# Mixer of a two-layer decoder step on one core: sample selection ahead of the prompt heads, layer norm moved, tanh for silu, rotations on TensorE

## The chip, the core and the metric

One core of a Trainium2 chip runs the whole step as one program. TensorE (PE) multiplies, VectorE (DVE), ScalarE (ACT) and GpSimd (POOL) work elementwise, SyncE (SP) issues most of the transfers; they run side by side and wait for each other through semaphores. The metric is the device time of one execution in microseconds (us); less is better. Three runs of the kernel before took 1205.79, 1207.03 and 1207.75 us (median 1207.03).

## The reference

Two layers work on 264 tokens: 256 of a prompt and one new token of each of 8 sequences ("samples") whose past of 1024 tokens lies in paged caches. Each layer is a gated feed-forward (SwiGLU), a mixer, and a second feed-forward, all with norms around them. Cut to the mixer, which is what changes:

```
a = u @ w_in                       # q, k, v, indexer q/k/weights, conv and pool inputs
q, k, qi, ki = partial_rope(...)   # x*cos + permuted(x)*sin
# convolution: depthwise, 31 taps, then
y = silu(layernorm(conv + bias)) @ conv_pw
# pooling: running means, then @ pool_w
# attention, prompt: indexer scores, top 64 of 256 per query, softmax over those, @ v
# attention, sample: indexer scores over 1025 keys, top 256, softmax over those, @ v
y = concat([conv, pool, attention]) @ w_out
```

All arithmetic is float32.

## The kernel before, in words

Activations lie transposed, features on the partitions, 264 tokens on the free axis, so one matrix unit is a 128x1024 tile of weights. Each such unit is loaded by SP into `raw`, rounded by ACT (`split`, L351) into `w_hi` and its rest computed by DVE (L556) into `w_lo`; PE then does three products for each of 8 blocks (L1001, L1002, L1003), 24 matmuls for one unit. A feed-forward has 66 units. The mixer has 16 units of input (numbers 0 to 15, of which 15 holds `conv_pw` and `pool_w`) and 8 of output.

The order of the work is written out by hand, once for each engine: each has a function `mixer(L)`, executed for both layers, and each engine works strictly through its own list. In the mixer:

- **Projections.** PE computes units 0 to 14 (`unit(m)`), DVE scales each by `rstd` as it leaves PSUM (`chunk`, L645). For the rotations PE multiplies the scaled tile by a permutation (`perm`, L1103), and DVE computes product with sine, product with cosine and sum (`rope`, L658, L659, L662). Between the units run the indexer scores and the search for the 256 largest of the 1025 sample scores, eight rounds of count on DVE (`count`, L716, L717) and sum over partitions on PE (`digit`, L1108).
- **Convolution.** 31 taps as small matmuls (`taps`, L1120) into four banks of PSUM, copied by ACT (L458) and added by PE (`fold`, L1131).
- **Attention.** The past keys come in two halves, `keys(0)` and `keys(1)` (L1235), because the tile `kv` holds 4 of 8 sequences; the second half can be loaded only when PE has used the first (semaphore `k_used`). The values are `values(0)` from a tile `vx` and `values(1)` from `kv` (L1324). The prompt's 8 heads go in four rounds j of two heads: `scores(j)` on PE (L1248, L1249), `masked(j)` on DVE (L859 to L863), `exps(j)` on ACT (L471), `norm(j)` on DVE (L870), transposes on PE (L1271), copies on ACT (L485), the product with the values on PE (L1282, L1283), and two copies out on ACT and DVE (L487, L892).
- **After the four rounds** come the layer norm of the convolution (L1297, L1301, L930, L932), the softmax over the sample's scores (L919 to L928, L491), transposes (L1308), the values, the silu (L501), the products with `conv_pw` and `pool_w`, and the output matrix: `half_out(0)` and `half_out(1)` first with 4 of 8 blocks each, the rest once the attention is there.

SP's list around the attention: when unit 14 is done, 8 transfers of values for one sequence into `vx` (`first_values`, L265), 32 of keys into `kv` (`batch`, L252, wait for `k_used`), 8 more into `vx`, 32 of values into `kv`, and then weights again. POOL issues 16 more transfers into `vx` (L1454) and computes the pooling.

Of the kernel before, what the change touches and what calls it, by code (L numbers as in the profile page):

```python
# [14 lines left out]
AL = mybir.AluOpType  # L15
# [67 lines left out]
    tanh=2, glu=2, stack=1, diag=2, conv=1, c_part=4, c_fold=1, conv_p=1, c_sum=1, c_cent=1, c_sq=1, c_var=1, c_rms=1, c_norm=1, c_silu=1,  # L83
# [9 lines left out]
def build(nc, xT, wts, par, cst, ptab, digits, kT, vC, kxT, scT, spT,  # L93
          yT, okT, ovT, okiT, ocP, ocS, opP, opS):
    ctx = ExitStack()
    with ctx:
# [20 lines left out]

        s1 = [at[0] + 4 * KD * NT]
# [33 lines left out]

        qi = place("qi", [128, 2, NT], F32, s1)
# [18 lines left out]
        rtmp = place("rtmp", [128, 2, NT], F32)  # L172
# [3 lines left out]
        kn = place("kn", [128, 4], F32)  # L176
        best = place("best", [128, 8], F32)
# [49 lines left out]
        CONV_BANKS = (3, 4, 5, 7)  # L227
# [9 lines left out]
        def _(sp):  # L237
# [42 lines left out]
            for L in range(DEPTH):  # L280
# [65 lines left out]
        def _(act):  # L346
# [69 lines left out]
            def mixer(L):  # L416
# [6 lines left out]
                for m in range(3, 7):  # L423
                    split(L, u0 + m)
                tanh(0)
# [18 lines left out]
                split(L, u0 + 11)  # L444
                act.wait_ge(sem["v_t"], at_layer(L, "v_t", 1))
                act.activation(vn[:, :, :], PS[:, 6, 128:384].rearrange(
                    "p (a b) -> p a b", a=2), ACT.Copy).then_inc(sem["v_nat"], 1)
                for m in range(12, 18):
                    split(L, u0 + m)

# [13 lines left out]
                ins.then_inc(sem["conv_p"], 1)  # L464

# [10 lines left out]
                exps(0)  # L476
                for j in range(4):
                    if j < 3:
                        exps(j + 1)
                    for a in range(2):  # L480
                        act.wait_ge(sem["p_t"], at_layer(L, "p_t", 2 * j + a + 1))
                        if j:

                            act.wait_ge(sem["o_p"], at_layer(L, "o_p", j))
                        act.activation(pT[:, a, :], PS[:, (7, 0)[a], 0:384], ACT.Copy).then_inc(sem["p_tc"], 1)  # L485
                    act.wait_ge(sem["o_p"], at_layer(L, "o_p", j + 1))
                    act.activation(h_hi[:, 4 + j, 0:NP], PS[:, 1, 0:NP], ACT.Copy).then_inc(sem["o_hi"], 1)  # L487
                act.wait_ge(sem["c_cent"], at_layer(L, "c_cent", 1))
                act.activation(csq[:, :, :], cacc[:, :, :], ACT.Square).then_inc(sem["c_sq"], 1)
                act.wait_ge(sem["s_smax"], at_layer(L, "s_smax", 1))  # L490
                act.activation(psm[:, :], psm[:, :], ACT.Exp, scale=SCALE,  # L491
                               bias=smx[:, 1:2], accum_out=smx[:, 2:3]).then_inc(sem["p_sexp"], 1)
                act.wait_ge(sem["c_var"], at_layer(L, "c_var", 1))
                act.activation(crs[:, :], PS[:, 1, 0:NT], ACT.Sqrt, scale=1.0 / 256, bias=epsb[:, 0:1]).then_inc(sem["c_rms"], 1)
                act.wait_ge(sem["p_st"], at_layer(L, "p_st", 1))
                act.activation(pTs[:, :, :].rearrange("p c (q r) -> p c q r", q=4),
                               PS[:, 6:8, :].rearrange("p a b -> p (a b)").rearrange(
                                   "p (c q x) -> p c q x", c=NPG, q=4)[:, :, :, 0:16], ACT.Copy).then_inc(sem["p_stc"], 1)
                act.wait_ge(sem["c_norm"], at_layer(L, "c_norm", 1))
                for c in range(2):  # L500
                    ins = act.activation(cacc[:, c, :], cacc[:, c, :], ACT.Silu,  # L501
                                         scale=pars[:, LNG + c:LNG + c + 1], bias=pars[:, LNB + c:LNB + c + 1])
                ins.then_inc(sem["c_silu"], 1)
                act.wait_ge(sem["c_silu"], at_layer(L, "c_silu", 1))
                act.activation(cp_hi[:, :, :], cacc[:, :, :], ACT.Copy).then_inc(sem["c_hi"], 1)
                act.wait_ge(sem["pool_y"], at_layer(L, "pool_y", 1))
                act.activation(pl_hi[:, :, :], pw[:, :, :], ACT.Copy).then_inc(sem["pl_hi"], 1)
                act.wait_ge(sem["c_out"], at_layer(L, "c_out", 1))
                act.activation(h_hi[:, 0:2, :], PS[:, 4:6, 0:NT], ACT.Copy).then_inc(sem["c_ohi"], 1)
                act.wait_ge(sem["unit_done"], at_layer(L, "unit_done", u0 + N_IN))  # L510
                for c in range(2):
                    ins = act.activation(h_hi[:, 2 + c, :], PS[:, 6 + c, 0:NT], ACT.Copy,
                                         scale=pars[:, PSC + c:PSC + c + 1])
                ins.then_inc(sem["pl_ohi"], 1)
                act.wait_ge(sem["v_used"], at_layer(L, "v_used", 2))
                for q in range(4):
                    ins = act.activation(osb[32 * q:32 * q + 8, :, :], PS[32 * q:32 * q + 8, 2:4, 0:128], ACT.Copy)
                ins.then_inc(sem["o_sc"], 1)
                split(L, u0 + 18)
                act.wait_ge(sem["o_ms"], at_layer(L, "o_ms", 1))  # L520
                act.activation(h_hi[:, 4:8, NP:], ms[:, :, :], ACT.Copy).then_inc(sem["o_shi"], 1)
# [26 lines left out]
        def _(dve):  # L548
# [88 lines left out]
            def mixer(L):  # L637
                u0 = U_MIX
                perms, ropes = [0], [0]
# [11 lines left out]
                def rope(x, bank, own=None):  # L651

                    perms[0] += 1
# [952 lines left out]
```

## Time and profile before

| | |
|---|---|
| runs, us | 1205.79, 1207.03, 1207.75 |
| the profiled execution, us | 1206.3 |
| its span (first to last instruction), us | 1204.8 |
| mean granted clock of TensorE | 0.96 |
| busy, share of the span | PE 92%, PEld 87%, DVE 64%, ACT 45%, POOL 17% |

A timeline row gives start, length, engine, line of the kernel, operation, what is written and read, how many instructions, and in brackets how long the engine stood idle before it and what released it. PE is recorded twice, as matmuls (PE) and as weight loads (PEld). An f32 matmul is recorded as two instructions, one on float32r data (a rounded part) as one. PEclk is the granted clock in parts of full speed: 1.00 is 2.4 GHz, 0.50 is 1.2 GHz. The first layer's mixer runs from 221.3 to 389.5 us, the second's from 811.5 to 979.7 us.

### The profile page before, as it was taken

What the parts mean: (1) busy time and instruction counts of PE and PEld (TensorE: products, weight loads), DVE (VectorE), ACT (ScalarE), POOL (GpSimd) and SP (SyncE); (2) the same over time, 40 slices, a digit from 0 to 9 for tenths busy, and PEclk for the clock granted to TensorE, in tenths of its full rate; (3) what the DMA queues carried; (4) which work ended last, traced back from release to release, by engine and by line L of the source; (5) the groups of instructions that cost most, each with busy time, mean ns of one, the idle gap of its engine ahead of it and who ended that gap; (6) DMA issues with size and microseconds to landing.
All of it is one profiled execution on the core that took longest, in us unless ns stands there. A gap on an engine that the chain in (4) does not pass through costs nothing.

```text
span 1204.8 us, 28977 instructions
## 1 busy us (share of the span) xinstructions
PE 1104.7 (92%) x9500; PEld 1044.8 (87%) x9500; DVE 774.2 (64%) x1244; ACT 541.6 (45%) x866; POOL 209.2 (17%) x233
## 2 busy tenths in 40 slices
PE   5999999978679999999989999999786799999997
PEld 4999999867348899999989999998663699999996
DVE  3766644789954766664466666457998466666546
ACT  4444434532345544443454444345223555444436
POOL 3211100210510312110031111011215021211002
PEclk9999999998869999999999999999896799999999
DMA  7454566343454355555435456553425434555551
GB/s 248 170 202 174 194 230 226 113 132 103 94 141 138 105 175 185 181 186 181 158 91 195 175 197 225 204 192 113 127 80 116 131 123 158 177 188 177 188 175 39
DMA packets 92302, 192.96 MB, mean 160 GB/s; under 512 B 12338, under 2 KB 50418, under 8 KB 92098
## 3 DMA queue, kind: packets, MB, share of 16 engines
q1 hardware_dynamic: 89730, 187.44, 46.9%
q0 software_dynamic: 2496, 4.55, 1.6%
q8 instruction: 42, 0.69, 0.2%
q14 instruction: 34, 0.28, 0.1%
HBM read 189.35 MB, written 2.59 MB: 159 GB/s over the span
## 4 chain that ended last, share of the span: by engine, by line
PE 47%; issue 39%; DVE 5%; POOL 3%; ACT 2%; POOLq 2%; DMA 1%; DVEq 0%; SPq 0%; ACTq 0%
PE PS L1001 14%; PE PS L1002 14%; PE PS L1003 14%; PE PS L1035 2%; DVE w_lo L556 1%; POOLq L1453 1%; PE PS L1047 1%; PE PS L1050 1%; PE PS L1046 1%; POOL h L1412 1%; ACT w_hi L351 1%; DVE wk L680 1%; POOL vx L1454 1%; DMA raw<-in_wts 1%; DVE wk L691 0%
## 5 line engine op out<-in xcount | busy, mean ns | idle before, releaser
L556 DVE TENSOR_TENSOR w_lo<-raw,w_hi 128x1024 fp32r<-128x1024 f32 x312 | 413.2, 1324 | 315.3 <-ACT w_hi L351 312.9
L1001 PE MATMUL PS<-x_hi,w_hi 128*128 128x264 f32 x1552 | 448.7, 289 | 10.5 <-DVE w_lo L556 10.5
L351 ACT ACTIVATE w_hi<-raw 128x1024 fp32r<-128x1024 f32 x312 | 328.3, 1055 | 267.5 <-PE PS L1003 264.3
L1002 PE MATMUL PS<-x_lo,w_hi 128*128 128x264 f32 x1552 | 445.0, 287 | 0.0
L1003 PE MATMUL PS<-x_hi,w_lo 128*128 128x264 f32 x1552 | 444.7, 287 | 0.0
L1001 PEld LDWEIGHTS PS<-x_hi,w_hi 128*128 128x128 f32 x1552 | 297.6, 192 | 11.7 <-DVE w_lo L556 11.3
L1002 PEld LDWEIGHTS PS<-x_lo,w_hi 128*128 128x128 f32 x1552 | 297.7, 192 | 0.1
L1003 PEld LDWEIGHTS PS<-x_hi,w_lo 128*128 128x128 f32 x1552 | 296.1, 191 | 0.0
L1001 PE MATMUL PS<-h_hi,w_hi 128*128 (+1 forms) x832 | 237.3, 285 | 3.4 <-issue 3.0
L1003 PE MATMUL PS<-h_hi,w_lo 128*128 (+1 forms) x832 | 237.1, 285 | 0.0
L1002 PE MATMUL PS<-h_lo,w_hi 128*128 (+1 forms) x832 | 236.4, 284 | 0.0
L1401 POOL TENSOR_TENSOR us<-gs,us 128x264 f32<-128x264 f32 x88 | 95.2, 1082 | 434.1 <-DVE us L607 434.1
L1001 PEld LDWEIGHTS PS<-h_hi,w_hi 128*128 128x128 f32 x832 | 156.6, 188 | 4.3 <-issue 4.3
L1002 PEld LDWEIGHTS PS<-h_lo,w_hi 128*128 128x128 f32 x832 | 157.1, 189 | 0.0
L1003 PEld LDWEIGHTS PS<-h_hi,w_lo 128*128 128x128 f32 x832 | 156.7, 188 | 0.0
L392 ACT ACTIVATE gs<-gs 128x264 f32<-128x264 f32 x88 | 37.3, 424 | 199.6 <-DVE gs L601 199.6
L1412 POOL TENSOR_TENSOR h<-h,y 128x264 f32<-128x264 f32 x48 | 41.6, 901 | 389.7 <-DVE y L587 389.7
L601 DVE TENSOR_TENSOR gs<-PS,rstd 128x264 f32<-128x264 f32 x88 | 38.1, 433 | 26.7 <-PE PS L1003 21.1
L1035 PE MATMUL PS<-sq,con 128*128 128x264 f32 x96 | 31.3, 409 | 14.7 <-ACT sq L534 13.8
L615 DVE TENSOR_TENSOR h_lo<-us,h_hi 128x264 f32 x88 | 37.6, 427 | 0.0
L607 DVE TENSOR_TENSOR us<-PS,rstd 128x264 f32<-128x264 f32 x88 | 37.5, 426 | 0.0
L397 ACT ACTIVATE h_hi<-us 128x264 f32 x88 | 36.0, 409 | 2.8 <-POOL us L1401 2.8
(262 smaller groups left out, 981.8 us busy)
## 6 DMA issues: line engine op xcount, KB each, us to landing
raw<-in_wts SPq DMA_DIRECT2D x315, 512.0 KB, 3.8
kv<-in_kT SPq DMA_DIRECT2D x128, 64.0 KB, 2.0
kx<-in_kxT SPq DMA_DIRECT2D x128, 32.0 KB, 2.1
kv<-in_vC SPq DMA_DIRECT2D x64, 64.0 KB, 1.9
vx<-in_vC SPq DMA_DIRECT2D x32, 64.0 KB, 2.7
vx<-in_vC POOLq DMA_DIRECT2D x32, 64.0 KB, 2.2
h<-in_xT SPq DMA_DIRECT2D x1, 1056.0 KB, 4.9
out_yT<-h SPq DMA_DIRECT2D x8, 132.0 KB, 1.8
```

The lines of the kernel that those rows point to most:

```text
L351: act.activation(w_hi[:, u % SPLIT, :], raw[:, u % RAW, :], ACT.Copy).then_inc(sem["w_hi"], 1)
L392: act.activation(gs[:, f % 3, :], gs[:, f % 3, :], ACT.Silu).then_inc(sem["silu"], 1)
L556: tt(w_lo[:, u % SPLIT, :], raw[:, u % RAW, :], w_hi[:, u % SPLIT, :].bitcast(F32), AL.subtract).then_inc(sem["w_lo"], 1)
L601: tt(gs[:, f % 3, :], PS[:, 2 * (f % 3), 0:NT], rstd[:, :], AL.mult).then_inc(sem["gs"], 1)
L607: tt(us[:, f % 3, :], PS[:, 2 * (f % 3) + 1, 0:NT], rstd[:, :], AL.mult).then_inc(sem["us"], 1)
L615: tt(out, us[:, f % 3, :], hi.bitcast(F32), AL.subtract).then_inc(sem["h_lo"], 1)
L1001: pe.matmul(out, w_hi[:, w, cols], hi, start=start, stop=False)
L1002: pe.matmul(out, w_hi[:, w, cols], lo, start=False, stop=False)
L1003: return pe.matmul(out, w_lo[:, w, cols], hi, start=False, stop=stop)
L1035: pe.matmul(PS[:, 7, 0:NT], ones, sq[:, ORDER[i], :], start=(i == 0), stop=(i == KD - 1)).then_inc(sem["mm_pre"], 1)
L1401: pool.tensor_tensor(us[:, f % 3, :], gs[:, f % 3, :], us[:, f % 3, :], AL.mult).then_inc(sem["mid"], 1)
L1412: pool.tensor_tensor(h[:, d, :], h[:, d, :], y[:, d, :], AL.add).then_inc(sem["h_new"], 1)
```

## The change

- **Rotations.** DVE computes `turn` = rstd times cosine and rstd times sine once per mixer, and each chunk that is rotated leaves PSUM as two products into `part`. PE adds them by two matmuls into one bank, with the identity and with the permutation. ACT copies the sum out. DVE's three operations for each rotation are gone.
- **PE's order after unit 14.** `keys(0)` comes ahead of the taps, the layer norm's two sums stand between `scores(0)` and `keys(1)`, the sample's selection, softmax, transposes and values go between the first two rounds of the prompt's heads, and the products with `conv_pw` and `pool_w` between the later rounds. The last rounds stand right ahead of the output matrix.
- **DVE and ACT** follow in the same order. The last four rounds of eight-fold maxima for the prompt's selection are split around the sample's ties.
- **Silu** is written as x/2 * (1 + tanh(x/2)), with the halves of gain and bias in `half_ln`; the tables for square root and exponential are called for ahead of their use.
- **SP** loads both sequences of `vx` first, then the keys.
- **Banks** of PSUM: the convolution takes 3, 7, 0, 1; transposes 7 and 5; head outputs 6; sample values 4; the other mixers' outputs 0 and 1.

```
-        CONV_BANKS = (3, 4, 5, 7)
+        CONV_BANKS = (3, 7, 0, 1)
@@ sync
                 first_values(L, 0, places)
+                first_values(L, 1, places)
                 for q in range(KV):
                     batch(kT, L, q, places[2 * q + 1], "k_used", q + 1)
-
-                first_values(L, 1, places)
                 for q in range(KV):
                     batch(vC, L, q, places[2 * q + 1], "k_used", KV + q + 1)
@@ scalar
+                def rope(x, bank):
+                    ropes[0] += 1
+                    act.wait_ge(sem["perm"], at_layer(L, "perm", ropes[0]))
+                    act.activation(x, PS[:, bank, 0:NT], ACT.Copy).then_inc(sem["rope"], 1)
...
+                warm(0, ACT.Sqrt)
+                act.wait_ge(sem["c_cent"], at_layer(L, "c_cent", 1))
+                act.activation(csq[:, :, :], cacc[:, :, :], ACT.Square).then_inc(sem["c_sq"], 1)
...
-                for c in range(2):
-                    ins = act.activation(cacc[:, c, :], cacc[:, c, :], ACT.Silu,
-                                         scale=pars[:, LNG + c:LNG + c + 1], bias=pars[:, LNB + c:LNB + c + 1])
+                for c in range(2):
+                    ins = act.activation(cacc[:, c, :], cacc[:, c, :], ACT.Identity,
+                                         scale=half_ln[:, c:c + 1], bias=half_ln[:, 2 + c:3 + c])
+                ins.then_inc(sem["c_tanh"], 1)
+                act.wait_ge(sem["c_tanh"], at_layer(L, "c_tanh", 1))
+                act.activation(csq[:, :, :], cacc[:, :, :], ACT.Tanh).then_inc(sem["c_tanh"], 1)
@@ vector
-                def rope(x, bank, own=None):
-                    perms[0] += 1
-                    dve.wait_ge(sem["perm"], at_layer(L, "perm", perms[0]))
-                    tmp = rtmp[:, ropes[0] % 2, :]
-                    if ropes[0] >= 2:
-                        dve.wait_ge(sem["rope"], at_layer(L, "rope", ropes[0] - 1))
-                    tt(tmp, PS[:, bank, 0:NT], con[:, C_SIN:C_SIN + NT], AL.mult)
-                    b = step(L, tt(x, x if own is None else own, con[:, C_COS:C_COS + NT], AL.mult))
-                    after(L, b)
-                    ropes[0] += 1
-                    tt(x, x, tmp, AL.add).then_inc(sem["rope"], 1)
+                def products(m, also=()):
+                    slot = turns[0] % 2
+                    if turns[0] >= 2:
+                        dve.wait_ge(sem["perm"], at_layer(L, "perm", turns[0] - 1))
+                    turns[0] += 1
+                    src = PS[:, 6 if m == 2 else m % 2, 0:NT]
+                    chunk(m, *also, *((part[:, slot, i, :], src, (1.0, turn[:, i, :])) for i in range(2)))
...
+                for i, at_ in enumerate((C_COS, C_SIN)):
+                    k = step(L, tt(turn[:, i, :], rstd[:, :], con[:, at_:at_ + NT], AL.mult))
+                after(L, k)
...
+                dve.wait_ge(sem["c_tanh"], at_layer(L, "c_tanh", 2))
+                stt(cacc[:, :, :], csq[:, :, :], 1.0, cacc[:, :, :], AL.add, AL.mult).then_inc(sem["c_silu"], 1)
@@ tensor
-                def perm(m, x, bank, which=C_PERM):
+                def perm(m, bank, own=C_ID, other=C_PERM):
                     pe.wait_ge(sem["chunk"], at_layer(L, "chunk", m + 1))
-                    return pe.matmul(PS[:, bank, 0:NT], con[:, which:which + 128], x, start=True, stop=True)
+                    slot = turns[0] % 2
+                    turns[0] += 1
+                    for i, which in enumerate((own, other)):
+                        ins = pe.matmul(PS[:, bank, 0:NT], con[:, which:which + 128], part[:, slot, i, :],
+                                        start=(i == 0), stop=(i == 1))
+                    ins.then_inc(sem["perm"], 1)
...
+                digit(5)
+                pe.wait_ge(sem["chunk"], at_layer(L, "chunk", 15))
+                keys(0)
+                taps(0, 2)
+                digit(6)
+                taps(2, 2)
+                digit(7)
+                taps(4, 4)
+                fold()
+                scores(0)
...
+                keys(1)
...
+                scores(1)
+                pe.wait_ge(sem["dg"], at_layer(L, "dg", 1))
...
+                softmax_t(0)
+                scores(2)
...
+                values(0)
+                mixed(0)
+                values(1)
+                softmax_t(1)
+                scores(3)
+                mixed(1)
+                softmax_t(2)
...
+                mixed(2)
...
+                softmax_t(3)
+                mixed(3)
```

In the new code `softmax_t(j)` are round j's transposes and `mixed(j)` its products with the values.

How the instructions stand now. First PE, from the last projection on; `dgw` and `gp` are the taps, `kv` and `LA` the past keys and the samples' queries, `ak` and `aq` the prompt's keys and queries. Before:

```order
L1120 MATMUL PS<-gp,dgw 32x256 x64
L1108 MATMUL PS<-rad,con 128x1
L1120 MATMUL PS<-gp,dgw 32x256 x96
L1108 MATMUL PS<-rad,con 128x1
L1120 MATMUL PS<-gp,dgw 32x256 x88
L1107 REGISTER_ALU
L1108 MATMUL PS<-rad,con 128x1
L1131 MATMUL PS<-cpart,stack 32x512 x4
L1232 ISA
L1235 MATMUL PS<-kv,LA 32x512 x8
```

And now:

```order
L1264 MATMUL PS<-kv,LA 32x512 x8
L1157 MATMUL PS<-gp,dgw 32x256 x64
L1145 MATMUL PS<-rad,con 128x1
L1157 MATMUL PS<-gp,dgw 32x256 x64
L1144 REGISTER_ALU
L1145 MATMUL PS<-rad,con 128x1
L1157 MATMUL PS<-gp,dgw 32x256 x120
L1168 MATMUL PS<-cpart,stack 32x512 x4
```

The first half of the past keys moved from behind the fold to ahead of the taps.

Then PE around the second half of the past keys. Before, it stood in the third round of heads, between the transposes of `sp_` and the products of `pT` and `vn`:

```order
L1271 MATMUL PS<-con,sp__107 128x128 x6
L1232 REGISTER_ALU
L1235 MATMUL PS<-kv,LA 32x512 x8
L1282 MATMUL PS<-pT,vn 64x256
L1283 MATMUL PS<-pT,vn 64x128
```

Now it follows the layer norm's sums (`cacc`, `csq`), ahead of every softmax:

```order
L1336 MATMUL PS<-cacc,con 128x264 x2
L1340 MATMUL PS<-csq,con 128x264 x2
L1261 REGISTER_ALU
L1264 MATMUL PS<-kv,LA 32x512 x8
L1345 MATMUL PS<-ak,LA 32x1 x8
L1277 MATMUL PS<-ak,aq 128x256
```

Three rounds of transposes and products that stood ahead of it are behind it now.

And DVE at the mixer's start (`raw`, `w_hi` and `w_lo` are the weights' split). Before:

```order
L732 TENSOR_REDUCE stack<-con 128x32
L645 SCALAR_TENSOR_TENSOR qi<-PS,rstd 128x264
L555 REGISTER_ALU
L556 TENSOR_TENSOR w_lo<-raw,w_hi 128x1024
L645 SCALAR_TENSOR_TENSOR qi<-PS,rstd 128x264
```

Now:

```order
L767 TENSOR_REDUCE stack<-con 128x32
L771 TENSOR_TENSOR turn<-rstd,con 128x264 x2
L613 REGISTER_ALU
L684 SCALAR_TENSOR_TENSOR part<-PS,turn 128x264 x2
L594 REGISTER_ALU
L595 TENSOR_TENSOR w_lo<-raw,w_hi 128x1024
L684 SCALAR_TENSOR_TENSOR part<-PS,turn 128x264 x2
```

Two operations came in ahead of the first chunk, and each rotated chunk has two.

## Rows read from the trace of the kernel before

**Rows 1.** Busy time by stage, first layer: windows, then each engine's busy time.
```profile
core 0: us, PE busy (x) PEld busy (x) DVE busy (x) ACT busy (x) POOL busy (x), PEclk, DMA share, GB/s
...
311.00:344.00 33.00, 20.60 (x142) 11.47 (x132) 27.10 (x51) 13.16 (x46) 16.87 (x19) 0.69 0.57 111
364.00:390.00 26.00, 24.40 (x197) 24.16 (x198) 10.48 (x14) 13.33 (x24) 0.00 (x0) 1.00 0.42 143
```

**Rows 2.** PE in the projections, first layer: timeline.
```profile
263.41 0.71 PE L1103 MATMUL PS<-ak,con 128*128 128x264 f32 x2 [2.77 <-DVE ak L645]
...
273.29 0.56 PE L1108 MATMUL PS<-rad,con 128*128 128x1 f32 x2 [4.77 <-DVE rad L717]
...
279.38 0.28 PE L1108 MATMUL PS<-rad,con 128*128 128x1 f32 x2
...
292.45 0.38 PE L1108 MATMUL PS<-rad,con 128*128 128x1 f32 x2 [0.91 <-DVE rad L717]
```

**Rows 3.** DVE in the projections, first layer: timeline.
```profile
269.09 0.43 DVE L658 TENSOR_TENSOR rtmp<-PS,con 128x264 f32<-128x264 f32 x1
...
270.25 0.14 DVE L707 TENSOR_SCALAR rad<-rad 128x1 f32<-128x1 f32 x1
```

**Rows 4.** SP's issues around the attention, both layers: timeline.
```profile
296.03 4.79 SPq L265 DMA_DIRECT2D vx<-in_vC  x8
313.31 17.05 SPq L252 DMA_DIRECT2D kv<-in_kT  x32
340.49 16.41 SPq L252 DMA_DIRECT2D kv<-in_vC  x32
...
886.67 5.46 SPq L265 DMA_DIRECT2D vx<-in_vC  x8
```

**Rows 5.** The page's DMA issues: KB each, median us to landing.
```profile
kv<-in_kT SPq DMA_DIRECT2D x128, 64.0 KB, 2.0
```

**Rows 6.** PE from unit 14's end to the output matrix: timeline.
```profile
295.78 2.76 PE L1120 MATMUL PS<-gp,dgw 32*32 32x256 f32 x128
...
311.26 1.90 PE L1235 MATMUL PS<-kv,LA 128*32 128x512 f32 x16
...
316.33 1.23 PE L1248 MATMUL PS<-ak,aq 64*128 64x256 f32 x4 [2.32 <-DVE spm L863]
317.35 0.64 PE L1249 MATMUL PS<-ak,aq 64*128 64x128 f32 x4
...
321.55 1.54 PE L1271 MATMUL PS<-con,sp__107 128*128 128x128 f32 x6 [3.56 <-DVE sp__107 L870]
...
337.06 3.41 PE L1235 MATMUL PS<-kv,LA 128*32 128x512 f32 x16
...
341.21 0.88 PE L1271 MATMUL PS<-con,sp__107 128*128 128x128 f32 x6
...
355.08 3.60 PE L1324 MATMUL PS<-vx,pTs 128*8 128x128 f32 x64 [0.88 <-ACT pTs L496]
...
361.97 1.93 PE L1324 MATMUL PS<-kv,pTs 128*8 128x128 f32 x64
```

**Rows 7.** DVE during one head's round, and late in GpSimd's pooling: timeline.
```profile
320.47 1.03 DVE L870 TENSOR_TENSOR sp__107<-sp__107,sps 128x512 f32<-128x512 f32 x2
...
326.58 0.95 DVE L859 TENSOR_TENSOR sp__107<-PS,bias 128x768 f32<-128x768 f32 x1
...
328.61 0.45 DVE L863 TENSOR_SCALAR spm<-spm 128x4 f32<-128x4 f32 x1
...
332.37 3.16 DVE L870 TENSOR_TENSOR sp__107<-sp__107,sps 128x512 f32<-128x512 f32 x2
```

**Rows 8.** PE in the output matrix, first layer: timeline.
```profile
364.10 0.39 PE L1001 MATMUL PS<-h_hi,w_hi 128*128 128x264 f32 x1 [0.19 <-DVE h_lo L942]
...
369.00 0.36 PE L1001 MATMUL PS<-h_hi,w_hi 128*128 128x264 f32 x1 [1.51 <-issue]
...
389.47 1.94 PE L1022 MATMUL PS<-sq,con 128*128 128x264 f32 x8
```

More of the change, by code:

```diff
@@ L151, in build @@
         stp = place("stp", [128, 2, NB, PB + 1], F32)
+        turn = place("turn", [128, 2, NT], F32, s_heads)
+        part = place("part", [128, 2, 2, NT], F32, s_heads)
+        assert s_heads[0] <= s1[0]
         qi = place("qi", [128, 2, NT], F32, s1)
@@ L474, in exps, with heads_in @@
                     ins.then_inc(sem["p_exp"], 1)
[L476 to L479, printed above, removed]
+                def heads_in(j):
                     for a in range(2):
@@ L488, in mixer @@
[L488 to L494, printed above, removed]
@@ new lines, in mixer @@
+                act.wait_ge(sem["c_tanh"], at_layer(L, "c_tanh", 1))
+                act.activation(csq[:, :, :], cacc[:, :, :], ACT.Tanh).then_inc(sem["c_tanh"], 1)
+                exps(2)
+                act.wait_ge(sem["v_used"], at_layer(L, "v_used", 2))
+                for q in range(4):
+                    ins = act.activation(osb[32 * q:32 * q + 8, :, :], PS[32 * q:32 * q + 8, 4, 0:256].rearrange(
+                        "p (a b) -> p a b", a=2), ACT.Copy)
+                ins.then_inc(sem["o_sc"], 1)
@@ L513, in mixer @@
                                          scale=pars[:, PSC + c:PSC + c + 1])
                 ins.then_inc(sem["pl_ohi"], 1)
[L515 to L518, printed above, removed]
+                heads_hi(2)
+                heads_in(3)
+                heads_hi(3)
                 split(L, u0 + 18)
-                act.wait_ge(sem["o_ms"], at_layer(L, "o_ms", 1))
@@ L778, in mixer @@
                 split(L, u0 + 9)
-                plain(7, ak[:, :])
+                products(7)
                 top8()
@@ L928, in mixer @@
                 ts(heads(dg[:, :]), own_rows, psm[:, PAST:], None, AL.mult).then_inc(sem["dg"], 1)
+                masked(1)
+                norm(0)
                 dve.wait_ge(sem["c_rms"], at_layer(L, "c_rms", 1))
@@ L1251, in scores, with softmax_t @@
                     ins.then_inc(sem["s_p"], 1)
-                keys(0)
-                scores(0)
-                scores(1)
-                for j in range(4):
+                def softmax_t(j):
                     pe.wait_ge(sem["p_norm"], at_layer(L, "p_norm", j + 1))
@@ new lines, in mixer @@
+                keys(0)
[6 more added lines that the diff above has]
+                scores(0)
+                pe.wait_ge(sem["conv_p"], at_layer(L, "conv_p", 1))
+                pe.wait_ge(sem["conv_s"], at_layer(L, "conv_s", 1))
+                for c in range(2):
+                    ins = pe.matmul(PS[:, 1, 0:NT], ones, cacc[:, c, :], start=(c == 0), stop=(c == 1))
+                ins.then_inc(sem["c_sum"], 1)
@@ new lines, in mixer @@
+                pe.matmul(PS[:, 4, 256:320], ones, dg[:, :], start=True, stop=True)
+                values(0)
+                mixed(0)
[4 more added lines that the diff above has]
+                softmax_t(2)
+                pe.wait_ge(sem["o_sc"], at_layer(L, "o_sc", 1))
+                for c in range(2):
+                    ins = pe.transpose(PS[:, 4, 128 * c:128 * c + 128], osb[:, c, :], ident)
+                ins.then_inc(sem["o_st"], 1)
```

252 lines of the change are left out of this document (122 added, 130 removed).

## The prediction

> **What bounds the kernel now.** I read the table of windows by stage first, then who PE waited for, then PE's, DVE's and SP's timelines through the mixer. The chain that ended last is of little use here: between 296 and 395 us it follows GpSimd's transfers and pooling, for which nobody waits at its end.
>
> The feed-forwards are PE's: matmuls with a rounded operand start 0.12 us apart (from 369.00 to 389.47 us there are 168 of them, 20.47/168 = 0.122 us) [rows 8], and the change touches nothing there. The mixer isn't PE's. In the attention PE is busy 20.6 of 33 us, at 0.69 of its clock [rows 1], since it waits for DVE and, having waited, runs at the lower of its two levels, 1.2 GHz. So the question is the chain of waits through the mixer, twice, once for each layer. I cut the first layer's at two points: A up to the end of unit 14, 295.8 us; B from there to the first product of the output matrix, 364.1 us; C from there to 389.5 us [rows 6, 8]. B is 68.3 us and C 25.4 us. The second layer's SP row, 886.67 us, is the same place in a mixer that looks alike [rows 4], so what one layer gives counts twice.
>
> **A, the projections.** Three things work against each other.
> - At the start DVE must make two products for `turn`, and each rotated chunk has a second product. Chunk operations start 0.35 us apart (269.09 and 269.44 to 269.90 us lie between the two rows shown: three operations and a wait in 1.16 us) [rows 3]. Until the second chunk is out that is four more, about 1.5 us, and PE waits for it; two more f32 matmuls of 264 columns lie on PE itself, 0.44 us each by the distance of the rotation and the product behind it. Unit 3 starts about 1.9 us later. All that follows moves along, also the wait of 2.77 us for unit 7's chunk, where 0.3 us more comes on top [rows 2].
> - The rotation of `ak` stood between two parts of the count, 1.16 us [rows 3]. It is gone, and the first `digit` comes at +2.2 - 1.1 = +1.1 us against 273.29 us.
> - From the first to the fifth digit it took 292.45 - 273.29 = 19.2 us: 6.1 us for a unit at the low clock, 3.6, and twice about 4.75 us [rows 2], where DVE (split 1.2, chunk, rotation 1.16, digit, count) was the longer one. Now DVE has 4.75 - 1.16 + 0.35 = 3.95 us, PE 24 x 0.122 + 2 x 0.44 + 0.15 = 3.95 us, so all rounds at full clock take about 4.0: 6.5 + 3 x 4.0 = 18.5 us, 0.7 us less.
>
> The copies on ACT (0.4 us each, eight) lie in its idle time; if that cover were gone, one would add 0.4 us to a round. A: +0.4 us. Bounds: -2.4 (the clock stays up through unit 10, whose 24 matmuls then save 24 x 0.1) and +2.2 us (the start's delay is never won back).
>
> **B, the attention.** Here a queue of transfers takes the place of DVE. Before, the second keys were issued from 313.31 us on and used at 337.06 us, the second values from 340.49 us on and used at 361.97 us [rows 4, 6]: neither was waited for. Now, counted from unit 14's end:
> - SP issues both sequences for `vx` first: 4.8 to 5.5 us for 8 transfers, 9.2 for 16 (the second 8 had all buffers free and may be quicker). The first half of the keys is used by PE early, at about 2.5 us (it waits for the last projection's chunk and eight copies) + 1.9 us, so `k_used` holds nothing up. Then 32 key transfers in 17.1 us, the last of them landing 2.0 us after its issue, which is 0.5 us before the row's end: 9.2 + 17.1 + 1.5 = 27.8 us [rows 4, 5].
> - PE comes to `keys(1)` before that: 2.5 wait + 1.9 keys + 13.5 us of taps with digits (now at one stretch, so that the 2 us of copies are in full view) + 2 + 1.1 fold + 0.9 scores + 0.9 and 0.9 for the norm's sums with two waits of some 1.6 us comes to 26 to 27 us even where half of it runs at low clock. The transfer ends last by 1 to 4 us.
> - `keys(1)` after a wait runs at the low clock, 3.4 us as at 337.06 us [rows 6]. The values can be issued only now: 31.2 - 0.5 (the first of four sequences is free a little earlier) + 16.4 + 1.5 = 48.6 us [rows 4, 5].
> - Inside these 17.9 us lie the sample's softmax, two `masked`, one `norm`, eight transposes, `values(0)`; by the rows some 16.5 us. Under GpSimd's pooling DVE's norm took 3.16 us instead of 1.03 us [rows 7]; it would stand here, with the pooling still at about 323 to 335 us. Both sides come out close together.
> - The tail from `values(1)` on, at full and at low clock: values 1.9/3.6, transposes 0.9/1.5, scores(3) 0.8/1.7 [rows 6], `masked(3)` 2.2 (2.5 with its last row) and norm 1.2 on DVE [rows 7], transposes 0.9/1.5, osb's transposes 0.2/0.4, 12 products with `conv_pw` 1.5/2.9, ACT's copy of them and of `pT` with the waits 1.9, mixed(2) 0.8/1.6, 6 products 0.7/1.5, transposes 0.9/1.5, 0.5 wait, mixed(3) 0.8/1.6: 15.2 us and 23.6 us. Half of each gives 19.4 us.
>
> B is then 48.6 + 19.4 = 68.0 us against 68.3: -0.3 us. What was won by interleaving is taken by the two batches, which now stand on the path. Bounds: 27.8 + 1.9 + 17.4 + 15.2 = 62.3 (-6) and, each transfer at the slower 0.6 us of the rows for `vx`, 30.3 + 3.4 + 20.2 + 23.6 = 77.5 us (+9).
>
> The silu costs nothing that shows: one more ACT operation and one on DVE, between rounds of heads in which both wait. The same count of table loads is left, ahead of their use instead of in the chain.
>
> The Trainium skill (SBUF — State Buffer, the section on the shared port pair) says that DVE, with two SBUF inputs, and GpSimd exclude each other for a whole instruction. The 3.16 us row agrees. By that rule a norm in the pooling's time pays up to one GpSimd operation twice; without it B's middle part would be 2 us shorter, which the transfers would hide.
>
> **C, the output matrix.** Before, PE stopped 1.5 us after two half outputs, for the samples' part, which came last, and did two transposes for it [rows 8]. Now that part is finished before the last heads, and 192 products run through: 192 x 0.122 = 23.4 us against 25.4 us. C: -2.0 us; bounds 0 (the last head's remainder or split 18 is late by as much) and -2.0.
>
> **Sum.** +0.4 - 0.3 - 2.0 = -1.9 us for a layer, -3.8 us for both. The profiled execution took 1206.3 us, span 1204.8 us; the median is 0.7 us higher. 1207.0 - 3.8 = 1203.2 us; I say 1203.5 us.
>
> **The rivals.**
> - *The tail and everything ahead of it stay at the low clock.* For it: after waits of 2.3 and 3.6 us the transposes at 321.55 us take 1.54 us, at 341.21 us 0.88 us [rows 6], and the new order has a wait ahead of nearly every piece: for the keys, for `masked(0)` (about 5 us behind `keys(1)`: scores, sums, maximum, mask), for norm(2). Then B is 48.6 + 23.6 = 72.2 us, +3.9, and 2 x (0.4 + 3.9 - 2.0) = +4.6 us, 1211.6 us, slower than before. It decides once the tail is over 21.3 us, that is once three quarters of it run at 1.2 GHz. Against it: the values and transposes in a row give PE some 5 us without a pause. 28%.
> - *The transfers don't bind.* SP issues `vx` and keys without gaps in 0.5 us each and PE comes later than I think; the clock comes up in the tail. B 48.6 - 1.5 + 16.5 = 63.6 us (-4.7): 2 x (0.4 - 4.7 - 2.0) = -12.6 us, 1194.4 us. For it: the 16 `vx` transfers come at once here. Against: 48 issues before `keys(1)` are 24 us at the least. 22%.
> - *Nothing to see.* The change does what it says and the tail costs 21 us: within 2.4 us of before, 1206.5 us. 15%.
> - *My forecast*, 1199 to 1204.6 us: 35%.
>
> The Trainium skill (DMA: Bandwidth & Descriptors, on issuing from multiple engines) says issue time is usually small beside the transfer. The row of 32 transfers in 17.05 us speaks against it here [rows 4]. By the rule the two batches would leave the path, which is the second rival's case.
>
> **The numbers.** 0.2% of 1207 us is 2.4 us, about what can be told from no change. Faster by more: forecast 30 of its 35, second rival 22: 0.53. Within: 0.20, from the third rival and the edges. Slower: 0.27. The range for 8 in 10 is 1195 to 1213 us; that of the forecast alone is 1199 to 1206 us.
>
> **What would show it.** In the changed profile PE should stand idle ahead of `keys(1)` (L1264, second time) with a transfer, or nothing, named, 26 to 30 us after unit 14; the row of 32 value transfers should start within 1 us of `keys(1)`'s end; `values(1)` (L1317, second time) should follow the last of them within 2.5 us; the digits should be 4.0 us apart; no gap should be left among the 192 products at the end. It would be wrong if PE reached `keys(1)` after the keys had landed, if the digits stayed 4.75 us apart, or if the pause merely moved to the last head.

## The result and the profile after

| | before | after |
|---|---|---|
| median, us | 1206.06 (5 runs, 1203.57 to 1207.75) | 1215.38 (5 runs, 1212.73 to 1215.97) |
| profiled execution, us (span) | 1206.3 (1204.8) | 1212.95 (1211.4) |
| ratio | | 1.007, 95% interval 1.0055 to 1.0085 |

The change makes the kernel slower by some 9 us. The prediction said 1203.5 us, 1195 to 1213 us, faster with a chance of 0.53: wrong in sign and outside its range.

First the three stretches of the prediction, cut at the same places: the mixer's first sum, unit 14's end, the first product of the output matrix, and the sums after it.

| us | before, layers 1 and 2 | after, layers 1 and 2 | forecast of the difference |
|---|---|---|---|
| A | 74.6, 75.0 | 72.5, 74.5 | +0.4 |
| B | 68.3, 67.9 | 75.3, 74.6 | -0.3 |
| C | 25.4, 25.4 | 23.4, 23.4 | -2.0 |

The two mixers together are 7.3 us longer, the profiled span 6.6 us. Outside them the two profiles differ by +1.2 us ahead of the first mixer and -1.8 us between the two. The kernel before with a small edit in the attention alone (e4, below) shows such shifts too (222.44 us in place of 221.27 for the first mixer's start), so they aren't read as effects of the change. B is where the time went, 7 us a layer.

Inside B, the windows of the changed kernel: unit 14's end to `keys(1)`, to `values(1)`, to the output matrix, and then C (columns as in [rows 1]).
```profile
294.97:333.15 38.18, 22.46 (x544) 12.04 (x542) 24.57 (x70) 8.87 (x17) 20.12 (x29) 0.76 0.59 118
333.15:354.56 21.41, 12.14 (x137) 7.76 (x138) 15.49 (x30) 8.66 (x29) 0.00 (x0) 0.71 0.38 104
354.56:370.29 15.73, 11.12 (x135) 9.09 (x135) 9.00 (x22) 10.40 (x33) 0.00 (x0) 1.00 0.26 94
370.29:393.71 23.42, 23.42 (x193) 23.42 (x193) 10.13 (x11) 11.44 (x18) 0.00 (x0) 1.00 0.49 159
```
The prediction had 27.8, 20.8, 19.4 and 23.4 us. The first stretch is 10.4 us too long, the third 3.7 us shorter than said (its clock is 1.00). The last window has no idle time at all, where [rows 8] has a pause.

Who TensorE waited for in B (line, releaser, us in total, times, longest):
```profile
PE PS L1264 <- DMA kv<-in_kT: 8.2, 1, 8.2
PE PS L1277 <- DVE spm L884: 5.2, 1, 5.2
PE PS L1290 <- DVE sp__109 L891: 3.3, 2, 1.7
PE PS L1317 <- DMA kv<-in_vC: 2.5, 1, 2.5
```
The first line is new; in [rows 6] the second keys and the second values were waited for by nobody. TensorE's timeline, both layers:
```profile
297.29 3.12 PE L1264 MATMUL PS<-kv,LA 128*32 128x512 f32 x16 [2.20 <-issue]
...
333.15 3.64 PE L1264 MATMUL PS<-kv,LA 128*32 128x512 f32 x16 [8.25 <-DMA kv<-in_kT]
...
354.56 1.93 PE L1317 MATMUL PS<-kv,pTs 128*8 128x128 f32 x64 [2.50 <-DMA kv<-in_vC]
...
925.17 3.64 PE L1264 MATMUL PS<-kv,LA 128*32 128x512 f32 x16 [6.43 <-DMA kv<-in_kT]
```
And the transfers' issues, which answer to [rows 4]; then GpSimd's two output transfers of the pooling state:
```profile
296.42 9.93 SPq L269 DMA_DIRECT2D vx<-in_vC  x16
306.52 19.90 SPq L256 DMA_DIRECT2D kv<-in_kT  x32
336.77 16.16 SPq L256 DMA_DIRECT2D kv<-in_vC  x32
```
```profile
320.59 0.68 POOL L1498 DMA_DIRECT2D out_opP<-pp  x1 [0.28 <-issue]
321.17 1.28 POOL L1499 DMA_DIRECT2D out_opS<-stp  x1
```
The last key is issued at 326.1 us, but the wait ends only at 333.15. The DMA view of 321 to 331 us says why (busy share of the 16 DMA engines and GB/s in 40 slices of 0.25 us; median us to landing):
```profile
DMA  6643733132749999319989799989999699699899
GB/s 205 215 111 98 188 89 105 25 18 20 98 144 255 276 212 141 10 4 37 18 16 33 39 41 49 78 53 47 92 80 59 43 64 125 94 137 90 123 146 109
...
q1 hardware_dynamic: 1625, 0.74, 83.4%
q0 software_dynamic: 112, 0.20, 13.1%
...
kv<-in_kT SPq DMA_DIRECT2D x11, 64.0 KB, 7.2
out_opS<-stp POOLq DMA_DIRECT2D x1, 120.0 KB, 10.3
```
From some 324.75 us on the DMA engines are busy at nine tenths and move only 4 to 146 GB/s; eleven keys issued in the window land after a median of 7.2 us. The two queue rows give packets, MB and the time of the packets as a share of the 16 engines. q0's 0.20 MB are GpSimd's three transfers (15, 120 and 64 KB), so most of the busy time is booked on SyncE's packets (83.4%), which take longer, and not on those of the output. Where on their way the two collide the record doesn't say. The keys' own line shows it stretch by stretch: issues from 300 to 320 us (shortest, median and longest issue in ns; landing in us), then from 322 to 327 us.
```profile
L256 SPq DMA_DIRECT2D kv<-in_kT x20: 345/346/1652, 306.5 to 319.4; - x20
DMA to landing us min/median/max: 1.8/2.1/3.3
...
DMA to landing us min/median/max: 4.1/7.4/7.9
```
The kernel before has the same jam in the same place; its keys issued from 321 to 331 us:
```profile
DMA to landing us min/median/max: 1.9/6.5/9.2
```
But there they are used at 337.06 us [rows 6].

So step B's first sum, term by term (layer 1): SyncE starts 1.5 us after unit 14's end; 16 `vx` 10.1 us (said 9.2); 32 keys 19.9 (said 17.1); from the row's end to the use 6.7 (said 1.5). Together 38.2. In the second layer it is 0.2 + 9.0 + 20.4 + 7.1 = 36.7.

### The profile page after: what moved, and what is told of

It reads as the page before. It is cut to its first block, busy times and chain, and to the rows that moved or that the text cites. A ratio compares the mean times of both kernels' runs of the same rounds, so it can differ in the third digit from the quotient of the medians.

```text
span 1211.4 us, 29025 instructions
## 1 busy us (share of the span) xinstructions
PE 1104.9 (91%) x9528; PEld 1045.8 (86%) x9528; DVE 761.3 (63%) x1222; ACT 546.5 (45%) x890; POOL 206.8 (17%) x233
## 4 chain that ended last, share of the span: by engine, by line
PE 49%; issue 39%; DVE 4%; POOL 3%; ACT 2%; POOLq 2%; DVEq 1%; DMA 1%; SPq 0%; ACTq 0%
PE PS L1031 14%; PE PS L1032 14%; PE PS L1033 14%; PE PS L1065 2%; POOLq L1493 1%; PE PS L1138 1%; PE PS L1077 1%; PE PS L1076 1%; PE PS L1080 1%; POOL h L1451 1%; DVE w_lo L595 1%; DVEq L724 1%; DVE wk L715 1%; ACT w_hi L354 1%; DMA raw<-in_wts 1%
## 5 line engine op out<-in xcount | busy, mean ns | idle before, releaser
L1031 PE MATMUL PS<-x_hi,w_hi 128*128 128x264 f32 x1552 | 448.0, 289 | 10.3 <-DVE w_lo L595 10.3
L1031 PEld LDWEIGHTS PS<-x_hi,w_hi 128*128 128x128 f32 x1552 | 296.8, 191 | 11.7 <-DVE w_lo L595 11.2
L640 DVE TENSOR_TENSOR gs<-PS,rstd 128x264 f32<-128x264 f32 x88 | 38.1, 433 | 27.2 <-PE PS L1033 21.8
```

The costliest lines, as they stand in the source:

```text
L640: tt(gs[:, f % 3, :], PS[:, 2 * (f % 3), 0:NT], rstd[:, :], AL.mult).then_inc(sem["gs"], 1)
L1031: pe.matmul(out, w_hi[:, w, cols], hi, start=start, stop=False)
```

## The experiments

Medians of the runs. The runs of the kernel before that were taken beside them had medians of 1206.5 to 1207.3 us, and each ratio is to those taken beside it. k1 and v1 are the starts of `keys(1)` and `values(1)` after unit 14's end, tail from `values(1)` to the output matrix, all for the two layers of the profiled run.

| kernel | median, us | ratio to before, 95% | k1 | v1 | tail |
|---|---|---|---|---|---|
| after | 1215.38 | 1.0055 to 1.0085 | 38.2, 36.7 | 59.6, 58.3 | 15.7, 16.3 |
| e1 outputs late | 1206.74 | 0.9965 to 1.0014 | 31.7, 32.3 | 53.4, 53.9 | 18.0, 18.6 |
| e2 keys first | 1197.35 | 0.9895 to 0.9943 | 27.7, 36.2 | 49.5, 57.5 | 15.9, 17.1 |
| e3 both | 1197.14 | 0.9884 to 0.9939 | 27.8, 30.2 | 47.7, 50.4 | 16.9, 17.3 |
| e4 before, outputs late | 1205.82 | 0.9976 to 1.0009 | 40.1, 41.2 | 65.0, 66.1 | 2.1, 2.1 |
| e5 packed output | 1204.21 | 0.9971 to 1.0006 | 32.9, 31.5 | 54.6, 52.7 | 16.1, 15.7 |
| e6 Silu table | 1202.06 | 0.9942 to 0.9975 | 29.6, 29.6 | 49.3, 50.3 | 19.6, 20.2 |
| e7 rotations on VectorE | 1205.45 | 0.9968 to 1.0004 | 30.2, 30.1 | 50.4, 51.8 | 17.3, 17.1 |
| e8 first three on VectorE | 1195.14 | 0.9890 to 0.9948 | 30.2, 28.2 | 50.2, 48.2 | 17.3, 16.9 |
| e9 reordered | 1192.11 | 0.9868 to 0.9901 | 28.0, 27.1 | 51.0, 48.6 | 15.8, 14.4 |
| e10 ScalarE issues vx | 1193.70 | 0.9859 to 0.9910 | 28.6, 28.3 | 49.7, 51.3 | 14.4, 15.8 |
| e11 split early | 1194.44 | 0.9876 to 0.9929 | 27.2, 28.6 | 48.7, 51.6 | 14.5, 15.8 |

**e1, the outputs late.**
```diff
-                pool.dma_start(opP[...], pp[:, :, NP:]).then_inc(stored, 16)
-                pool.dma_start(out4(opS), stp[:, :, :, 1:]).then_inc(stored, 16)
...
                 pool.tensor_tensor(pw[:, :, :], pw[:, :, :], xp[:, :, :], AL.subtract).then_inc(sem["pool_y"], 1)
+                pool.wait_ge(sem["v_used"], at_layer(L, "v_used", 2))
+                pool.dma_start(opP[...], pp[:, :, NP:]).then_inc(stored, 16)
+                pool.dma_start(out4(opS), stp[:, :, :, 1:]).then_inc(stored, 16)
```


> The changed kernel with GpSimd's two output transfers of the pooling state (out_opP, out_opS) moved from ahead of the pooling to behind the last values(1); nothing is left out. In the changed kernel out_opS is issued at 321.2 us and lands after 10.3 us; the key transfers issued in those microseconds land after 7 to 8 us where the others take 2, and TensorE waits 8.25 and 6.43 us for them. Theory A (that one transfer holds up the keys): the last key lands some 2 us after its issue at 326.1 us, so keys(1) starts 4.5 to 5 us earlier in each layer, the values follow by as much, and the time is 1206 us (1204 to 1208) against 1215.4. Theory B (it is SyncE's queue, with sixteen vx transfers ahead of the keys; out_opS only happens to lie there): the keys land no earlier than 331 us and the time stays within 2 us of 1215.4. Theory C (keys(1) is not what binds; the chain of DVE or the low clock behind it is): the wait at keys(1) shrinks, but values(1) or the tail takes it back, 1213 to 1216 us.

Measured 1206.74 us, 8.6 less than the changed kernel. Theory A holds: `keys(1)` comes 6.5 and 4.4 us earlier, and the time is in its range, while those of theories B and C are missed. Moved to where it meets no key, the transfer itself still lands after 9.1 and 9.5 us. TensorE still waits:
```profile
305.20 20.36 SPq L256 DMA_DIRECT2D kv<-in_kT  x32
```
```profile
327.18 3.58 PE L1264 MATMUL PS<-kv,LA 128*32 128x512 f32 x16 [3.98 <-DMA kv<-in_kT]
...
918.69 3.64 PE L1264 MATMUL PS<-kv,LA 128*32 128x512 f32 x16 [4.39 <-DMA kv<-in_kT]
```
305.20 + 20.36 + 1.6 = 327.2: these 4 us are SyncE's queue alone.

**e5, the same transfer in large pieces.** This asks what makes it slow.
```diff
+                dve.tensor_copy(packed[:, :, :, :], stp[:, :, :, 1:])
...
-                pool.dma_start(out4(opS), stp[:, :, :, 1:]).then_inc(stored, 16)
+                pool.dma_start(opS[...].rearrange("a p c b k -> p (a c b k)"),
+                               packed[...].rearrange("p c b k -> p (c b k)")).then_inc(stored, 16)
```


> The changed kernel with everything in its place, out_opS at 321 us too, but read from a packed copy: VectorE copies the 15 of 16 columns that go out (480 numbers a partition) into a tile of their own, so that a partition's 1,920 bytes lie in one piece on both sides and not in 32 pieces of 60 bytes. Same bytes, same queue, same moment. Theory A1 (the many small pieces fill the 16 DMA engines): out_opS lands within 3 us, the keys within 2 to 3 us of their issue, keys(1) starts some 4.5 us earlier in each layer, and the time is 1206 to 1208 us, as with the transfer moved away. Theory A2 (it is the write itself, or GpSimd's queue): it still takes 9 us or more and the time stays at 1214 to 1217 us.

The sizes in that text are a slip: 120 KB over 128 partitions are 960 bytes each (240 numbers), in 16 pieces of 60 bytes, 2,048 pieces in all. The DMA view of 875 to 955 us and, from the one of 285 to 365 us, the same transfer:
```profile
out_opS<-packed POOLq DMA_DIRECT2D x1, 120.0 KB, 3.5
```
```profile
out_opS<-packed POOLq DMA_DIRECT2D x1, 120.0 KB, 3.1
```
10.3 us have become 3.1 and 3.5, and the keys' median is back at 2.1. 1204.21 us, as good as moving it away. So it is the small pieces: the bytes, the target and the queue are the same in both. The Trainium skill (DMA: Bandwidth & Descriptors, Specifications) gives 512 bytes as the least for full rate; that agrees with 960 against 60 bytes here, though where the limit lies no run shows.

**e2 and e3, the keys first.**
```diff
-                first_values(L, 1, places)
                 for q in range(KV):
                     batch(kT, L, q, places[2 * q + 1], "k_used", q + 1)
+                first_values(L, 1, places)
```


> The changed kernel with SyncE issuing the second sequence's eight vx transfers behind the 32 keys, as the kernel before has it, and not ahead of them. The keys are then issued about 4.9 us earlier, 301.5 to 321.5 us, just ahead of out_opS. Theory A: the keys escape out_opS, land by 324 us, TensorE comes to keys(1) at 324.9 us without a wait, and both layers win all of their 8.25 and 6.43 us: 1200 to 1203 us. Theory B: the same 4.9 us a layer and no more, 1205 to 1207 us. Theory C: 1213 to 1216 us.

> Both edits together: keys ahead of the second vx, and the two output transfers behind values(1). Theory A: the keys are in time by either edit, so it is the same as with the keys first alone, 1200 to 1203 us, at most 1 us less since the eight vx transfers and the values find free queues. Theory B: the same as with the keys first alone. Theory C: 1213 to 1216 us. If it is well under the keys-first kernel, out_opS costs something at a second place.

Both at 1197 us, 18 less than the changed kernel and 9 less than before, and 3 to 6 us under what theory A had said. Part of that is `values(1)`, which waits less as well (2.50 and 0.95 us in the changed kernel, 0.34 us and nothing in e3). e2 escapes the jam only just. Its profiled run (1206.06 us, the slowest of its six) was caught in the second layer: SyncE's last keys went out up to 910.1 us, the output transfer at 908.93, and they landed after up to 8.9 us.
```profile
908.93 1.28 POOL L1499 DMA_DIRECT2D out_opS<-stp  x1
```
```profile
919.12 3.64 PE L1264 MATMUL PS<-kv,LA 128*32 128x512 f32 x16 [6.60 <-DMA kv<-in_kT]
```
In the first layer of the same run it was issued at 324.10 us, after the last key, and nobody waited. In e3 nothing holds up `keys(1)` in either layer, and its five runs lie within 1193.74 and 1198.11 us.

**e4, the same for the kernel before** (the control; the same two lines moved).

> The kernel before with the same two output transfers moved behind the last values product. There key transfers issued from 320 to 330 us landed after 5 to 9 us too, but they were used only at 337.06 us, with no wait. Theory A: no change, 1206 us within 1.5, since nobody waits for a key there. If it gains 3 us or more, out_opS was on the path before the change as well, and A's account of the difference is wrong.

1205.82 us: no change. The keys issued from 321 to 331 us, which landed after 1.9/6.5/9.2 us in the kernel before, land here after
```profile
DMA to landing us min/median/max: 1.7/1.9/2.2
```
So the jam was there before the change, came from the same transfer, and cost nothing; the change moved the use of the keys into it.

**e6, the Silu table again, on e3.**
```diff
                 for c in range(2):
-                    ins = act.activation(cacc[:, c, :], cacc[:, c, :], ACT.Identity,
-                                         scale=half_ln[:, c:c + 1], bias=half_ln[:, 2 + c:3 + c])
...
-                act.activation(csq[:, :, :], cacc[:, :, :], ACT.Tanh).then_inc(sem["c_tanh"], 1)
+                    ins = act.activation(cacc[:, c, :], cacc[:, c, :], ACT.Silu,
+                                         scale=pars[:, LNG + c:LNG + c + 1], bias=pars[:, LNB + c:LNB + c + 1])
...
-                stt(cacc[:, :, :], csq[:, :, :], 1.0, cacc[:, :, :], AL.add, AL.mult).then_inc(sem["c_silu"], 1)
```


> The kernel with keys first and the outputs late (1197.1 us) with the sample branch's silu taken from the Silu table again, in place of half-scale, tanh and (1+t)x. Two ACT_TABLE_LOADs of 1.28 us come back, to Silu and back to Exp ahead of exps(2), inside the heads' rounds; one ACT operation of 0.64 us and one of DVE of 0.71 us go. My reading of the profile: exps(2) is late by 1.3 to 2.6 us, and DVE's norm(2) and all behind it move along: +1.3 to +2.6 us for a layer, 1200 to 1202.5 us. Rival (ACT's time there is slack, as the prediction took the whole silu edit to be): within 1 us of 1197.1 us.

1202.06 us, 4.9 more than e3 and in the range, and the rival is out. ScalarE's timeline:
```profile
344.23 1.28 ACT L528 ACT_TABLE_LOAD   x1
345.53 1.10 ACT L528 ACTIVATE cacc<-cacc,pars 128x264 f32<-128x264 f32 x2
346.65 1.28 ACT L498 ACT_TABLE_LOAD   x1
347.94 0.51 ACT L498 ACTIVATE sp__109<-sp__109,spm 128x256 f32<-128x256 f32 x1
```
The two loads stand between two heads' exponentials, and the tail grows from 16.9 and 17.3 to 19.6 and 20.2 us. With the sample branch in the middle of the heads the tanh form is worth 2.5 us a layer.

**e7 and e8, the rotations, on e3.** e7 puts all eight back on VectorE (the old `rope`, one product each), e8 only the first three, with `turn` made behind `glu(0)`.

> The same kernel with all eight rotations on VectorE again, as the kernel before has them; the two turn products, the second product per chunk and ScalarE's copies are gone. By the prediction's step A and the traces since: the start is earlier by 1.7 us, the rotation of ak stands between the parts of the count again (+1.16), digits are 4.8 us apart in the DVE-bound rounds and not 4.0, and behind unit 14 the wait for the eighth rotation's copy is other. Theory A (A costs about the same by either way, 74.0 against 74.6 us in the profiles so far): +0.5 us a layer, 1198 us. Rival (TensorE's rotations are what makes the mixer fast): +2 us a layer or more, 1201 us. Rival (they cost): 1195 us or less.

> The same kernel with the first three chunks' rotations on VectorE (as before) and the five later ones on TensorE; the turn products are made at 248 us, where VectorE waits for 2.8 us. The 1.7 us that the start lost are won back unless the wait at unit 7 takes them, since VectorE's index sums come 1.7 us earlier too: A 72.3 us, 1193.7 us. Rival (the late start is absorbed by a later wait): 1197 us.

e7 costs 8.3 us, so theory A fell. With all rotations on VectorE nothing clear of noise is left of this order's gain over the kernel before (ratio 0.9968 to 1.0004). Only about 0.8 us a layer of it lies in A (74.6 and 75.5 against 74.0 and 74.5 us). The rest comes behind: `LA` is built behind the eighth rotation, and `keys(0)` starts 3.3 us after TensorE's last work in place of 2.2:
```profile
299.98 3.47 PE L1286 MATMUL PS<-kv,LA 128*32 128x512 f32 x16 [3.29 <-issue]
```
Its share of the 8.3 us isn't settled: the two mixers of the profiles differ by 5.7 us, the rest of the span by 0.8. e8 gains 2.0 us of the 3.4 expected; the first digit comes 1.7 us earlier in both layers, counted from the mixer's start. The medians of e3 and e8 are 2 us apart with runs that overlap, so this gain is likely, not shown by the times alone.

**e9 to e11, a better kernel.** e9, on e8: `chosen` and the bias ahead of the convolution's mean, `masked(0)` ahead of the sample's softmax, `norm(0)` beside its exp, `keys(1)` ahead of the variance, `values(1)` behind `mixed(1)`.

> A try for a better kernel, on the one of 1195.1 us (first rotations on VectorE). There VectorE idles 4.5 us ahead of the convolution's mean and is then busy without a pause from 320.4 to 331.9 us, and all that follows hangs on it. Moved: the choice by rank and the prompt's bias (some 4.8 us) ahead of the mean, masked(0) ahead of the sample's softmax and norm(0) into the time of its exp, keys(1) on TensorE ahead of the variance, values(1) behind mixed(1) with the samples' transposes behind the first output products. If VectorE's chain binds: some 3.5 us for a layer, 1188 us. If the transfers bind (the keys land at +27, the values 16.3 us after keys(1) and 4 more for vx): within 1.5 us of 1195.

1192.11 us, 14.4 less than before: the best of the study, and less than half of what was hoped for. VectorE's idle time ahead of the mean fell from 6.3 and 5.3 us in e8 (the 4.5 us of the text above is e3's first layer) to 2.2 and 1.9 us:
```profile
321.56 0.77 DVE L946 SCALAR_TENSOR_TENSOR cacc<-PS,cacc 128x264 f32<-128x264 f32 x2 [2.23 <-PE PS L1356]
...
325.83 1.22 DVE L952 SCALAR_TENSOR_TENSOR psm<-Z,PS 128x1024 f32<-128x1024 f32 x1 [1.30 <-PE PS L1365]
```
Counted from unit 14's end, `psm` starts at 31.4 and 30.5 us in place of 33.9 and 31.0 in e8. It could start earlier still, but it now waits 1.3 and 1.4 us for TensorE, since the scores that it needs stand behind `keys(1)`, and `keys(1)` waits for its keys (0.87 and 1.28 us). The transfers bind again.

> The same with the sixteen vx transfers that SyncE issued now issued by ScalarE, which idles for 16 us there. SyncE then has 64 issues in place of 80: the keys start at 298 us and not at 299.8, the values directly behind keys(1). If SyncE's queue binds: another 2 to 3 us for a layer, 1184 us. If issuing from a third engine slows SyncE's own issues by as much as it takes off: no change against the reordered kernel.

In e10 ScalarE issues sixteen `vx` with `act.dma_start`; that is no gain. The keys start at 300.38 us, not 298, and end no earlier than in e9 (the last row is e9's):
```profile
304.41 11.35 ACTq L476 DMA_DIRECT2D vx<-in_vC  x16
```
```profile
300.38 21.53 SPq L257 DMA_DIRECT2D kv<-in_kT  x32
```
```profile
299.95 20.63 SPq L257 DMA_DIRECT2D kv<-in_kT  x32
```
ScalarE takes 0.71 us for an issue and SyncE still 0.67 for a key. What SyncE waits for in front of the keys, in e9 and then in e10, says why the start didn't move:
```profile
SPq L257 <- PE PS L1284: 1.2, 1, 1.2
```
```profile
SPq L257 <- PE PS L1290: 3.5, 1, 3.5
```
Both lines of TensorE are `keys(0)`. The tile `kv` is free for the second keys only when the first have been used. In e9's first layer the batch already waited for that, and in its second layer `keys(0)` ended 0.1 us before the `vx` did, so a shorter queue ahead of the keys had nothing to win. The expectation overlooked this semaphore (`k_used`). Of SyncE's queue e10 shows only that its 32 key issues take no less time when sixteen others are gone.

> The kernel of 1192.1 us with unit 9's split and unit 7's products moved ahead of three of the four top8 rounds. In its profile that split of VectorE, with two operands in SBUF, takes 2.81 us beside GpSimd's dgw products (258.8 to 262.7 us) and 1.22 us elsewhere, and TensorE waits 3.1 us for what stands behind it. Theory A (the two engines shut each other out for such an operation, and the max and replace operations don't suffer): the split takes 1.2 us, TensorE's wait at unit 7 falls below 1 us, the first digit comes 1.6 us earlier in each layer: 1189 us. Rival (GpSimd's products now stretch the top8 rounds by as much): the sum of VectorE's work up to the first digit stays, 1192 us.

e11 is 2.3 us worse than e9 (the two ratios' intervals overlap), and its two layers show both outcomes. VectorE's split and GpSimd's products, layer 1 and then layer 2:
```profile
257.24 5.84 DVE L593 TENSOR_TENSOR w_lo<-raw,w_hi 128x1024 fp32r<-128x1024 f32 x1 [0.23 <-issue]
...
840.65 1.23 DVE L593 TENSOR_TENSOR w_lo<-raw,w_hi 128x1024 fp32r<-128x1024 f32 x1 [0.23 <-issue]
```
```profile
258.10 3.89 POOL L1499 TENSOR_TENSOR dgw<-stack,pars 128x992 f32<-128x992 f32 x2
...
842.11 3.76 POOL L1499 TENSOR_TENSOR dgw<-stack,pars 128x992 f32<-128x992 f32 x2
```
Where VectorE was done before GpSimd began, the split takes 1.23 us and the first digit comes 2.1 us earlier than in e9. Where they met it takes 5.84 us, and the digit comes 3.0 us later. In each such meeting VectorE's subtraction ends 1.1 us after GpSimd's second product (263.08 against 261.99 here; 265.92 against 264.83 in the changed kernel), as if it ran only then; here it had been started 0.9 us before the first product, while GpSimd was issuing a transfer. GpSimd's two products take 3.89 and 3.76 us, with VectorE's operation beside them or without. So VectorE is held up; that GpSimd is too, as theory A had it, no run shows. The place can't be chosen by order alone, it would take a wait.

## Why the prediction was wrong, point by point

- **A (+0.4 said, -2.1 and -0.5 found).** The mechanism held: the first digit at +53.05 us after the mixer's start, against +52.02 before (+1.0, said +1.1), then digits 4.02 us apart (said 4.0). The miss is the round behind the first digit, which I took at the low clock (6.5 us). It took 4.1 us in layer 1, the lower bound's case, and 5.6 in layer 2.
```profile
275.52 0.35 PE L1145 MATMUL PS<-rad,con 128*128 128x1 f32 x2 [2.98 <-DVE rad L752]
...
279.62 0.28 PE L1145 MATMUL PS<-rad,con 128*128 128x1 f32 x2
```
- **B, the last key's landing: the step that failed.** "The last of them landing 2.0 us after its issue" was the page's median over 128 key transfers [rows 5]. In this place it is 7 us in either kernel. The long landings stood in the trace of before, hidden behind a use at 337 us. The step should have asked what else is in the DMA engines in the microseconds to which the use is moved. Of the first sum's miss of 10.4 and 8.9 us this term is 5.2 and 5.6 us. e5 packs that one transfer and takes 11.2 us off; e1 moves it, together with the 15 KB one in front of it, and takes 8.6 us off.
- **B, SyncE's queue.** The reasoning was right (a queue of transfers takes DVE's place, `keys(1)` waits, the values start directly behind it and bind `values(1)`), the size was not: 19.9 to 21.7 us for 32 keys against 17.05 [rows 4]. In the changed kernel the 20 keys issued before 320 us take up to 1.65 us for a single issue, where 0.35 is the rule. I had the remedy in hand and didn't look at it as an edit: with the second eight `vx` behind the keys TensorE no longer waits for the queue (e3, and e2's first layer).
- **B, TensorE's arrival.** Said 26 to 27 us after unit 14, found 29.9 (333.15 - 8.25 - 294.97) and 30.3. This alone would have made B longer by 2 us. In e3, without a wait, it is 27.8 and 30.2.
- **B, the values and the tail.** 16.16 us for the values and 1.6 to their use, as said (16.4 and 1.5). The norm that was to be stretched by the pooling took 1.03 us, since GpSimd was done at 332 us. The tail, 15.7 and 16.3 us, ran at 2.4 GHz (1.00 in layer 1's window), as the lower bound of 15.2 had it, not at the mean of two levels. So the rival that gave 1211.6 us came nearest to the time for a wrong reason: its tail at the low clock isn't there. In the same way e5, the changed kernel without the jam, lies at 1204.2 us beside a forecast of 1203.5 only by luck: the way to `keys(1)` is still 5.1 and 3.7 us too long there, and the tail 3.3 and 3.7 us too short.
- **The rivals.** "The transfers don't bind" was close to what e3 reaches once the keys are first and the jam is gone: 1197.1 against 1194.4 us. My order of chances treated the queue's count as fixed. (By its parts, 0.30 and 0.22, the chance of faster is 0.52 and not 0.53.)
- **Silu.** "Costs nothing" held, but left out that it is worth 2.5 us a layer in this order.
- **C (-2.0).** Right: 23.42 us in both layers, no gap among the 192 products.

Measured less forecast, by the prediction's terms, layers 1 and 2: the way to `keys(1)` +10.4 and +8.9 us, from there to `values(1)` +0.6 and +0.7, the tail -3.7 and -3.1, A -2.5 and -0.9.

## What to carry to other kernels

When a use is moved earlier, look at its transfers' landing times in those very microseconds, not at their median, and at every other transfer in flight there, small outputs too. A transfer that nobody waits for still holds up those that somebody does; if its pieces are small, pack it or move it. And if a batch moves onto the path, its place in the queue is part of the change: here moving one line was worth 18 us, the jam that it escapes included, twice what the whole change lost. Then ask again what the batch itself waits for: in e9 and e10 its start hangs on the use that frees its tile, and less work in the queue ahead of it no longer helps.

## What the runs showed of the hardware

- 120 KB in 2,048 pieces of 60 bytes landed after 9.0 to 11.3 us wherever it was issued, and transfers of another engine's queue in that time landed after some 7 us in place of 2; packed to 960 bytes a partition it landed after 3.1 and 3.5 us.
- A VectorE subtraction of 1,024 columns with both operands in SBUF takes 1.22 us alone, and 2.81, 3.27 and once 5.84 us where it met GpSimd's products, each time ending 1.1 us after them. It stands ahead of TensorE's wait at unit 7 in the changed kernel too:
```profile
263.11 2.81 DVE L595 TENSOR_TENSOR w_lo<-raw,w_hi 128x1024 fp32r<-128x1024 f32 x1 [0.23 <-issue]
```
- SyncE's issues are 0.51 us apart in one batch and 0.62 to 0.68 in another. The long ones among the changed kernel's keys (over 0.8 us) fall between 307 and 316 us, mostly beside the small tap products on TensorE; but the batch of values has a long one too, of 1.47 us at some 348 us, where no taps run, and the batch of keys is as slow when sixteen other issues are taken off SyncE (e10). What lengthens them wasn't tried and stays open, and so does why SyncE starts 1.5 us after unit 14 in one layer and 0.2 us in the other.
